# Running the two context heads of a tile in turns, and loading a head's four gate matrices with one transfer

## What is computed

```python
def lru_coeffs(u2, p):
    gr = jnp.einsum("bnkhi,khij->bnkhj", uh, p["w_r"])      # gate r, per direction k and head h
    gi = jnp.einsum("bnkhi,khij->bnkhj", uh, p["w_i"])      # gate i
    r = jax.nn.sigmoid(gr + p["b_r"]); i = jax.nn.sigmoid(gi + p["b_i"])
    log_a = -LRU_C * r * jax.nn.softplus(-p["lam"])
    a = jnp.exp(log_a)
    bx = jnp.sqrt(-jnp.expm1(2.0 * log_a)) * (i * uf)
    return a, bx

# even_mixer on the context: only the last states are kept
xb_c = hc @ pe["w_in"][:, 3 * W_CONV:3 * W_CONV + W_LRU]
_, h_ctx = rglru_branch(xb_c, pe, h0, False)   # short conv of 4 taps, lru_coeffs, scan h = a*h + bx
out_x, _ = even_mixer(hx, h_ctx, pe)           # hx: RMS-normed, modulated x
```

## Time and profile before

| | us |
|---|---|
| time of the kernel before, median of 2 runs | 7019.85 |
| lowest and highest of these runs | 6962.27 and 7077.43 |
| the profiled execution, its own time | 6801.25 |
| its span on core 0, the slowest | 6800.0 |
| spans of the eight cores | 6772.1 to 6800.0 |
| busy: PE, DVE, ACT, POOL | 5158.1, 3728.1, 2904.4, 376.7 |

### The profile page before, as it was taken

The page is one execution under the profiler, slowest core; times in us unless marked ns, Lnnn a source line. Parts: engine busy times, 40 slices in busy tenths (PEclk is TensorE's granted clock), DMA queues, the critical chain, the costliest instruction groups (busy, mean ns, idle before and its releaser), DMA issues.

```text
span 6800.0 us, 77765 instructions; the slowest of 8 cores (6772.1 to 6800.0 us)
## 1 busy us (share of the span) xinstructions
PE 5158.1 (76%) x22504; PEld 2329.5 (34%) x22504; DVE 3728.1 (55%) x5180; ACT 2904.4 (43%) x4345; POOL 376.7 (6%) x595
## 2 busy tenths in 40 slices
PE   2488976797549987779845889688884689858887
PEld 1233333343323332334322333233342233323333
DVE  1466554856345555476534555547743565555674
ACT  1655553312465555331246555532125555553112
POOL 2100000000010000000001000000001000000000
PEclk9699998898669999889867999899985799989998
DMA  8211012132331101222233110212223210012221
GB/s 112 52 24 15 8 38 47 25 41 35 87 49 17 16 5 38 47 35 35 44 79 48 15 18 1 47 40 35 32 56 83 32 22 12 13 45 43 32 32 59
DMA packets 341728, 256.94 MB, mean 38 GB/s; under 512 B 45328, under 2 KB 307472, under 8 KB 341328
## 3 DMA queue, kind: packets, MB, share of 16 engines
q0 software_dynamic: 303232, 146.83, 17.5%
q1 hardware_dynamic: 28880, 71.58, 3.4%
q10 hardware_dynamic: 9216, 33.56, 1.2%
HBM read 365.17 MB, written 33.55 MB: 59 GB/s over the span
## 4 chain that ended last, share of the span: by engine, by line
PE 54%; DVE 21%; ACT 11%; issue 10%; DMA 4%; DVEq 1%; ACTq 0%; POOL 0%; POOLq 0%; SPq 0%
PE psall L112 54%; DVE arena L104 21%; ACT arena L104 10%; ACT L104 1%; DMA arena<-x 1%; DMA arena<-mod_w 1%; DMA out<-arena 1%; DVEq L68 1%; DMA arena<-ev_w_out 0%; DMA arena<-od_w_in 0%; ACTq L68 0%; POOL arena L104 0%; DMA arena<-ctx 0%; POOL arena L128 0%; POOLq L68 0%
## 5 line engine op out<-in xcount | busy, mean ns | idle before, releaser
L112 PE MATMUL psall<-arena 128*128 128x512 bf16 (+4 forms) x22504 | 5158.1, 388 | 1637.5 <-ACT arena L104 719.8
L112 PEld LDWEIGHTS psall<-arena 128*128 128x128 bf16 (+2 forms) x22504 | 2329.5, 107 | 4465.8 <-issue 2346.3
L104 ACT ACTIVATE arena<-arena 128x512 bf16<-128x512 f32 (+6 forms) x1683 | 1253.1, 764 | 901.3 <-DVE arena L104 586.2
L104 DVE TENSOR_TENSOR arena<-arena 128x512 bf16<-128x512 f32 (+10 forms) x922 | 720.4, 793 | 461.2 <-ACT arena L104 410.0
L104 ACT ACTIVATE arena<-psall,arena 128x512 f32<-128x512 f32 (+2 forms) x980 | 587.7, 650 | 750.9 <-PE psall L112 689.7
L104 DVE SCALAR_TENSOR_TENSOR arena<-psall,arena 128x512 f32<-128x512 f32 (+1 forms) x784 | 580.0, 749 | 577.8 <-PE psall L112 544.9
L104 ACT COPY arena<-psall 128x512 f32<-128x512 f32 (+1 forms) x664 | 375.6, 584 | 1129.3 <-PE psall L112 602.9
L104 DVE SCALAR_TENSOR_TENSOR arena<-arena 128x512 f32<-128x512 f32 (+5 forms) x818 | 711.2, 895 | 65.7 <-ACT arena L104 37.9
L104 DVE TENSOR_SCALAR arena<-arena 128x128 bf16<-128x128 f32 (+5 forms) x1490 | 480.8, 325 | 485.1 <-ACT arena L104 347.7
L104 ACT ACTIVATE arena<-psall 128x512 f32<-128x512 f32 x640 | 379.4, 595 | 830.1 <-PE psall L112 495.9
L104 DVE TENSOR_TENSOR_SCAN arena<-arena 128x1024 f32<-128x1024 f32 (+2 forms) x256 | 628.5, 2455 | 71.8 <-ACT arena L104 44.9
(11 more groups left out here) (12 smaller groups left out, 97.8 us busy)
## 6 DMA issues: line engine op xcount, KB each, us to landing
arena<-ev_w_in POOLq DMA_DIRECT2D x96, 512.0 KB, 6.5
arena<-x SPq DMA_DIRECT2D x64, 512.0 KB, 4.2
arena<-x SPq DMA_DIRECT2D x128, 256.0 KB, 2.6
arena<-od_w_in POOLq DMA_DIRECT2D x64, 512.0 KB, 5.8
out<-arena ACTq DMA_DIRECT2D x64, 512.0 KB, 2.6
arena<-ev_w_out POOLq DMA_DIRECT2D x32, 512.0 KB, 7.9
arena<-od_w_out POOLq DMA_DIRECT2D x32, 512.0 KB, 5.7
arena<-mod_w POOLq DMA_DIRECT2D x24, 512.0 KB, 13.4
```

What stands on the lines that cost most here:

```text
L104: ins = fn(**kw)
L112: ins = fn(**kw)
```

## The change

`ctx_unit` becomes a generator, `ctx_unit_g`, with a `yield` after each of its steps, and `run_rr` takes one step of each generator in turn. In each tile the x norm now comes first, then both gate sets are asked for, then the two heads run in turns: preparation of both, projection of both, taps of both, cast of both, direction 0 of both, direction 1 of both, the Sqrt of both, the scans. The four gate transfers of a head become one, from an input in which w_r and w_i are stacked by the host; in the slot the order is now (r, direction 0), (r, 1), (i, 0), (i, 1), and `gate_front` reads accordingly. The main heads use the same `load_gates`.

```diff
-    wr_d = dt_in("ev_w_r", [2, 8, 128, 128])
-    wi_d = dt_in("ev_w_i", [2, 8, 128, 128])
+    wri_d = dt_in("ev_w_ri", [2, 2, 8, 128, 128])
...
-            k.mm(P.matmul, [gwk, ubk], [pk], True, out=ps[:, 0:tw], lhsT=gwv[:, 2 * d, :], rhs=ubv[:, c0 + tl * tw:c0 + (tl + 1) * tw],
+            k.mm(P.matmul, [gwk, ubk], [pk], True, out=ps[:, 0:tw], lhsT=gwv[:, d, :], rhs=ubv[:, c0 + tl * tw:c0 + (tl + 1) * tw],
...
-            k.mm(P.matmul, [gwk, ubk], [pk], True, out=ps[:, 0:tw], lhsT=gwv[:, 2 * d + 1, :], rhs=ubv[:, c0 + tl * tw:c0 + (tl + 1) * tw],
+            k.mm(P.matmul, [gwk, ubk], [pk], True, out=ps[:, 0:tw], lhsT=gwv[:, 2 + d, :], rhs=ubv[:, c0 + tl * tw:c0 + (tl + 1) * tw],
...
-    def ctx_unit(j, jj, wA, kA, gwv, gwk):
+    def ctx_unit_g(j, jj, wA, kA, gwv, gwk):
...
         k.op("dve", V.memset, [], [CK("x")], ap=xbc[:, CTX + 2:CTX + 3], constant=0.0)
+        yield
...
         k.op("act", A.copy, [pk], [CK("x")], out=xbc[:, 2:2 + CTX], in_=ps[:, 0:CTX])
+        yield
...
+    def run_rr(gens):
+        gens = list(gens)
+        while gens:
+            for g in list(gens):
+                try:
+                    next(g)
+                except StopIteration:
+                    gens.remove(g)
...
-    def load_gates(j):
-        i = gw_state["n"] % 2
-        gw_state["n"] += 1
-        for d in range(2):
-            k.dma("pool", "gw%d" % i, out=gwf[i][:, 2 * d, :], in_=wr_d[d, j], reads=[], writes=[("gw", i)])
-            k.dma("pool", "gw%d" % i, out=gwf[i][:, 2 * d + 1, :], in_=wi_d[d, j], reads=[], writes=[("gw", i)])
+    def load_gates(j, slot=None):
+        i = gw_state["n"] % 2 if slot is None else slot
+        gw_state["n"] = i + 1
+        k.dma("pool", "gw%d" % i, out=gwf[i], in_=wri_d[:, :, j].rearrange("a d p m -> p (a d) m"), reads=[], writes=[("gw", i)])
         return gwf[i], ("gw", i)
...
-            for jj in range(2):
-                j = 2 * t + jj
-                if jj == 0:
-                    wA, kA = wget()
-                else:
-                    modulated_norm(lambda kc: X0.c(kc, tsl(t)), lambda kc: X0.key(kc, t), 512, 0, bi,
-                                   lambda kc: H0v[:, kc, tsl(t)], lambda kc: ("h0", kc, t))
-                gwv, gwk = load_gates(j)
-                ctx_unit(j, jj, wA, kA, gwv, gwk)
+            wA, kA = wget()
+            modulated_norm(lambda kc: X0.c(kc, tsl(t)), lambda kc: X0.key(kc, t), 512, 0, bi,
+                           lambda kc: H0v[:, kc, tsl(t)], lambda kc: ("h0", kc, t))
+            gws = [load_gates(2 * t + jj, slot=jj) for jj in range(2)]
+            run_rr([ctx_unit_g(2 * t + jj, jj, wA, kA, gws[jj][0], gws[jj][1]) for jj in range(2)])
```

More of the change, by code:

```diff
@@ L594, in ctx_unit @@
                        uc, CK("u"))
+            yield
         for d in range(2):
             k.op("act", A.activation, [CK("e%d" % d)], [CK("e%d" % d)], out=Ec[d], in_=Ec[d], func=AF.Sqrt, scale=-1.0)
+        yield
         for d in range(2):
             gate_back(d, TRc[d], CK("t%d" % d), Ec[d], CK("e%d" % d), HSc[d], CK("h%d" % d), 0.0, [])
+            yield
         k.op("dve", V.tensor_copy, [CK("h0")], ["hctx"], out=hctx[:, j, 0:1], in_=HSc[0][:, CTX - 1:CTX])
         k.op("dve", V.tensor_copy, [CK("h1")], ["hctx"], out=hctx[:, j, 1:2], in_=HSc[1][:, 0:1])
-    gw_state = {"n": 0}
-    def load_gates(j):
-        i = gw_state["n"] % 2
-        gw_state["n"] += 1
-        for d in range(2):
-            k.dma("pool", "gw%d" % i, out=gwf[i][:, 2 * d, :], in_=wr_d[d, j], reads=[], writes=[("gw", i)])
-            k.dma("pool", "gw%d" % i, out=gwf[i][:, 2 * d + 1, :], in_=wi_d[d, j], reads=[], writes=[("gw", i)])
+        yield
+    def run_rr(gens):
[6 more added lines that the diff above has]
+                    gens.remove(g)
+    gw_state = {"n": 0}
+    def load_gates(j, slot=None):
+        i = gw_state["n"] % 2 if slot is None else slot
+        gw_state["n"] = i + 1
+        k.dma("pool", "gw%d" % i, out=gwf[i], in_=wri_d[:, :, j].rearrange("a d p m -> p (a d) m"), reads=[], writes=[("gw", i)])
         return gwf[i], ("gw", i)
@@ L932 @@
         "ev_w_in": np.ascontiguousarray(inp["ev_w_in"][0], np.float32),
-        "ev_w_r": np.ascontiguousarray(inp["ev_w_r"][0], np.float32),
-        "ev_w_i": np.ascontiguousarray(inp["ev_w_i"][0], np.float32),
+        "ev_w_ri": np.ascontiguousarray(np.stack([inp["ev_w_r"][0], inp["ev_w_i"][0]]), np.float32),
         "ev_w_out": np.ascontiguousarray(inp["ev_w_out"][0], np.float32),
```

## The result

The changed kernel takes 0.9903 of the time of the kernel before, with a 95% interval of 0.9881 to 0.9925: about 1% faster, and clearly so. Its median is 6751 us.

What follows compares the result with a forecast made beforehand. A chain hopping between engines through ACT bounds the four context stages; 88.8 us saved there less 5.6 for TensorE's clock gives 83, ratio 0.9878, times the shown runs' median 7019.85 gives 6934 us, range 6700 to 7025.

Steps and rivals of the forecast that it cites:

- The pair: Two heads of a context tile, run in turns: 15.69 us for what took 20.56, a gain of 4.87 us.
- Fence wait: End of a context stage: ACT's wait for DVE's last copy grows from 2.72 to about 4.8 us.
- the likeliest case: Forecast with its unknown parts bounded: gain of about 50 to 105 us, 0.9926 to 0.9846 of before.
- within: Outcome that the changed kernel's time differs from before by no more than about 2%; chance 0.84.
- TensorE's clock behind the fence: Main part's first 16 tap matmuls run at the lower clock: 1.4 us lost a sample, 5.6 in all.
- the slack of x: Context tiles: third and fourth x pieces land 4.2 us after request, leaving 4.5 us before ACT copies.
- Rival 2: Context tiles: x pieces stay late, copies keep their 1.5 us gap; 24 us lost, 59 gained; chance 0.08.
- the gate transfers: Gate sets on the POOL queue: asked for about 39 us before use, so merging them was priced at nothing.
- Rival 4: Main part's start: the gate chain was on the path, 55 us more go, 138 in all; chance 0.09.
- rival 3: Context heads: they run one behind the other, only table loads go; 41 us gained; chance 0.03.
- rival 5: Context heads: a table switch costs more than its row; 17 us more go, 100 in all; chance 0.02.
- rival 6: Context tiles: slower through late third and fourth x pieces; landing 14 us after issue cancels all 83 us; chance 0.04.

## Why the prediction was right and where it was wrong

**What was right.** The mechanism and most of its terms. A tile was to take 39.2 us: 39.15 in the tile shown (copies 0.4 longer, norm and pair 0.3 and 0.2 shorter than summed up), 38.7 to 40.2 in the twelve that don't end a stage. The pair was to take 15.69: 15.52. Two CAST 1.7 us apart: 1.70. Fence wait 4.8: 4.77. Table loads 186: 186. Against the profiled execution's own 6801.25 us the sum gave 6718; core 0 went to 6703.8 from 6800.0, and 0.9903 lies within the 0.9846 to 0.9926 of the likeliest case.

**Wrong: "I scale their median: 7019.85 x 0.9878 = 6934".** Measured 6751. I had seen that the two runs stood 2.4 and 4.1% above the profiled execution and took them as the kernel's level all the same. Eight further executions of before show that its level is the profile's: the lowest took 6795.5, three more 6800.8 to 6801.1, and the other four lie higher, as the two of the table do (6866 to 7295). With the ratio that I forecast, 6801 would have given 6718. The step that failed is the choice of the base; it moved the forecast by 216 us, more than twice the whole effect. The 6751 lies within the range of 6700 to 7025 only because that range took in the spread of the executions.

**Wrong: "about 2% is what a measurement of this kernel can tell from no change".** The interval of the ratio is 0.2% wide to either side, and a gain of 1% stands out by four times that. I took the spread of all executions (6801 to 7077) for the error of a comparison. By the sum itself, a gain of 1.2% with bounds of 0.7 and 1.5%, the likeliest outcome was a kernel measurably faster, and 0.84 for "within" hid that.

**Mis-sized: "The four stages are 1.6 us longer on average than this one; I count none of that as gain".** Some 0.9 of the 1.6 lay at the copies, which waited for x (tile 0 of sample 0 took 47.8 us, those of samples 1 and 2 43.8 and 44.2); the rest is spread over heads and norm. The changed kernel has stages of 161.0 to 163.0, mean 161.8 against the 161.6 forecast for each, so that the 1.6 came back in full: 94.5 us in place of 88.8.

**Mis-sized: TensorE's clock behind the fence, 1.4 us a sample.** The taps take 21.8 us in the four samples against 20.1 before (5.92, 3.63, 5.23 and 5.30), so 0.4 a sample, 1.7 in all. I had expected 6 to 7 us each; they took 5.0 to 6.25, at a granted clock of 0.57 to 0.71, so not at the lower level throughout. I had weighed two rows of before, and one of them was the only one that ran at 3.6; the other two samples, at 5.2 and 5.3, would have told me that there was little left to lose. From the forecast of 83 us to the 96 measured, 5.7 are the longer stages and 3.9 the smaller loss at the taps; 3.4 more lie elsewhere outside the stages, where single stretches of the changed kernel differ by more between cores (the first takes 1489.8 us on core 0 and 1481.8 on core 1), and I put them down to nothing.

**Mis-sized: the slack of x, 4.5 us.** About 2 remain: the third piece was to be there 6 us after the first Tanh, and came 8.2 after it. I had taken the landing of 4.2 over, although gate sets and the weight block now move at the same time; in tiles 1 and 2 the third and fourth piece land after 5.8 and 7.5 us (means of cores 0 to 3), with four chained transfers after 3.6 and 4.7. It cost little here (on core 0 up to 1.1 us of gaps in the copies of a tile), and the kernel with x twice shows how near it was. Rival 2, late pieces, did not come true, but it describes well the kernels without the turns.

**Wrong in sign: "I price it at nothing", the gate transfers.** I asked only whether PE waits for a gate set, and it doesn't, before or after. What I did not ask is what stands behind the chain in the queue. There a 512 KB block waits, and without the chain it runs beside the pieces of x: 15 us slower in the old order (756.6 for 741.5), and about 4 in the new one (the means of 647.7 and 643.6, which no ratio backs). Rival 4, a gain from the shorter chain, falls with that: the stretches between the stages are 1485.5 us long on average before and 1485.8 after. By the rule of **DMA: Bandwidth & Descriptors** of the Trainium skill (section Rules for kernel authors), many small transfers should be made one large one; the run with one transfer alone, at 1.0023 (1.0007 to 1.0039), speaks against it for a chain that is off the path.

**The other rivals.** No overlap (rival 3) was tried on its own: the shared tables without turns give 749.9 us, so the loads alone do not carry the gain. A dearer table switch (rival 5) falls with the 15.52 us of the pair and with tile 0 of the kernel with shared tables. Slower by late x (rival 6) asked for 5.2 us more a tile to cancel the gain; doubling the transfers of x gives 5.8, so that twice the traffic of x would have been enough, and not only the 14 us of landing that I had named.

## What to carry to other kernels

Where a stage is a chain that hops between engines and none of them is full, list the gaps of the engine that takes part in most hops, and put independent work into them; the turns filled the gaps of one head with the other, and the idle time of DVE and ACT in the norm was worth 81 us more. A transfer that nobody waits for may still pace its queue: before it is made shorter, look at what large transfer stands behind it and what that will run beside. And take the base of a forecast from the execution whose rows it is built on, and the resolving power from the interval of a comparison, not from the spread of all runs.

## What the runs showed of the hardware that I had not expected

- One transfer of 128 KB takes 0.75 us of POOL to issue where one of 32 KB takes 0.53, and lands in 3.7 us (median) against 2.1. A chain of four took 11.3 us (9.2 and 2.1 to land), and it was the better neighbour.
- The 16 taps of PE behind 8.2 to 9.0 us without work took 5.0 to 6.25 us (granted clock 0.57 to 0.71), hardly more than behind 4.0 to 4.3 (5.2 to 5.9, clock 0.60 to 0.69); behind 2.1 to 2.4 and once 3.47 they took 3.62 and 3.63, at 1.00.
- A 512 KB block asked for 5 us ahead of the copies lengthens the landing of the fourth piece of x from 4.71 to 6.89 us, although the DMA engines are busy only 26 to 28% of the stage. That share is a mean: in the 12 us from 1908 of the kernel with one transfer, 19 of 40 slices of the profile stand at nine tenths or more.
